# Dilated attention in a hybrid decoder layer: far scores by residue class on column tiles, value products ahead of scores

## What is computed

```python
DIL_PAIRS = ((128, 1), (512, 4), (2048, 16))

def dilated_attention(q, k, v):
    """For pair (w, r) a query at t attends t, t-r, t-2r, ..., t-w.
    Branch outputs are merged with weights proportional to their softmax denominators."""
    for window, dil in DIL_PAIRS:
        o, lse = banded_causal_attention(to_stream(q), to_stream(k), to_stream(v), window // dil)
        ...
    w = jax.nn.softmax(jnp.stack(lses), axis=0)
    o = jnp.einsum('pbsh,pbshd->bshd', w, jnp.stack(outs).astype(jnp.float32))
```

## Time and profile before

| | |
|---|---|
| median of 3 runs | 507.02 us (506.67 to 508.36) |
| the profiled execution | 507.9 us, of it the span 505.4 us |
| PE busy | 489.3 us, 97% |
| DVE, ACT, POOL busy | 310.9, 227.4, 72.7 us |
| largest parts of PE's chain | output products (line 954) 16%, value products (line 913) 10%, input projection (lines 776 to 778) 24% |

### The profile page before, as it was taken

One profiled execution on the slowest core, in us unless ns is written; L12 is line 12 of the kernel. 1 busy time (PEld: TensorE's weight loads), 2 busy tenths in 40 slices (PEclk: granted clock), 3 DMA queues, 4 the chain that ended last, 5 costly groups with the idle time before them and its releaser, 6 DMA issues.

```text
span 505.4 us, 9699 instructions
## 1 busy us (share of the span) xinstructions
PE 489.3 (97%) x3480; PEld 448.2 (89%) x3480; DVE 310.9 (62%) x889; ACT 227.4 (45%) x512; POOL 72.7 (14%) x53
## 2 busy tenths in 40 slices
PE   4999999999999999999999999999999999999993
PEld 4999999999999988888888888899888888888882
DVE  4776645557574853434534468876767867787634
ACT  5633123112121134564545669946474655554640
POOL 0000000000000000111011100023232323231425
PEclk9999999999999999999999999999999999999998
DMA  8957272538633244432331357823342424241022
GB/s 284 377 160 205 89 245 83 172 122 266 210 110 112 95 138 134 133 94 90 95 95 49 97 173 238 247 58 105 110 137 63 149 56 151 64 145 45 3 81 83
DMA packets 51710, 67.82 MB, mean 134 GB/s; under 512 B 9553, under 2 KB 41297, under 8 KB 51665
## 3 DMA queue, kind: packets, MB, share of 16 engines
q1 hardware_dynamic: 51088, 66.17, 41.6%
q10 hardware_dynamic: 576, 1.05, 0.6%
HBM read 51.18 MB, written 16.02 MB: 133 GB/s over the span
## 4 chain that ended last, share of the span: by engine, by line
PE 90%; DMA 3%; DVE 3%; SPq 1%; ACT 1%; issue 1%; POOLq 0%; POOL 0%; ACTq 0%; DVEq 0%
PE long_ps L954 16%; PE o_ps L913 10%; PE wide L777 8%; PE wide L776 8%; PE wide L778 8%; PE long_ps L853 5%; PE long_ps L855 5%; PE wide L881 5%; PE narrow L893 5%; PE long_ps L854 5%; PE wide L882 4%; DMA q_pair<-q_spill 2%; PE wide L788 1%; PE wide L787 1%; PE wide L789 1%; PE narrow L931 1%
## 5 line engine op out<-in xcount | busy, mean ns | idle before, releaser
L776 PE MATMUL wide<-x_hi,w_hi 128*128 128x256 f32 x320 | 89.5, 280 | 0.3 <-DVE w_lo L1188 0.3
L777 PE MATMUL wide<-x_lo,w_hi 128*128 128x256 f32 x320 | 89.7, 280 | 0.0
L778 PE MATMUL wide<-x_hi,w_lo 128*128 128x256 f32 x320 | 89.4, 279 | 0.0
L776 PEld LDWEIGHTS wide<-x_hi,w_hi 128*128 128x128 f32 x320 | 60.2, 188 | 0.5 <-issue 0.4
L777 PEld LDWEIGHTS wide<-x_lo,w_hi 128*128 128x128 f32 x320 | 60.1, 188 | 0.0
L778 PEld LDWEIGHTS wide<-x_hi,w_lo 128*128 128x128 f32 x320 | 59.9, 187 | 0.0
L1035 ACT ACTIVATE spill<-turn 128x512 fp32r<-128x512 f32 x21 | 13.3, 632 | 103.3 <-DVE turn L1270 76.6
L1517 POOL TENSOR_TENSOR g_lo<-g_raw,g_hi 128x1024 fp32r<-128x1024 f32 x6 | 14.3, 2388 | 272.7 <-ACT g_hi L1040 272.7
L954 PE MATMUL long_ps<-wo_hi,y_hi 128*128 128x512 f32 x128 | 53.1, 415 | 0.0
L954 PE MATMUL long_ps<-wo_lo,y_hi 128*128 128x512 f32 x128 | 52.3, 408 | 0.0
L954 PE MATMUL long_ps<-wo_hi,y_lo 128*128 128x512 f32 x128 | 51.8, 404 | 0.0
(11 more groups left out here) (158 smaller groups left out, 1227.2 us busy)
## 6 DMA issues: line engine op xcount, KB each, us to landing
q_spill<-spill SPq DMA_DIRECT2D x32, 256.0 KB, 2.5
q_pair<-q_spill SPq DMA_DIRECT2D x128, 64.0 KB, 2.0
w_raw<-in_w_qkv SPq DMA_DIRECT2D x12, 512.0 KB, 5.3
x_raw<-in_x_t SPq DMA_DIRECT2D x16, 256.0 KB, 8.0
g_raw<-in_w_gate SPq DMA_DIRECT2D x8, 512.0 KB, 3.5
q_pair<-q_spill SPq DMA_DIRECT2D x32, 128.0 KB, 2.8
q_pair<-q_spill SPq DMA_DIRECT2D x128, 32.0 KB, 1.8
wo_raw<-in_w_out SPq DMA_DIRECT2D x8, 512.0 KB, 4.4
```

Source lines behind the costliest of these rows:

```text
L776: pe.matmul(dst, w_hi[s][:, k, f], t_hi[:, k, cols], start=(k == 0), stop=False)
L777: pe.matmul(dst, w_hi[s][:, k, f], t_lo[:, k, cols], start=False, stop=False)
L778: mm = pe.matmul(dst, w_lo[s][:, k, f], t_hi[:, k, cols], start=False, stop=(k == KT - 1))
```

## The change

- `score`: the far keys get products of their own, four per unit, one per class: 32 query columns (`q_whole`, unsplit fp32) times the keys of that class, read from k_b with a step of four elements, on the column tile of that class. Far and dense scores go to one PSUM bank, far ones first.
- POOL makes `q_whole` by adding the two halves of the query (`join_queries`), at the end of iteration v for unit v + 1; PE waits for it (`q_joined`).
- DVE masks far columns already in merged form with a mask that is gathered beforehand; the merge and its semaphore go.
- far value groups are cut at 96 rows where there are more than 128 (block 7: 96 and 96 instead of 128 and 64).
- `times_v(v - 3)` moves from the end of iteration v to its start, ahead of the scores, and `unit_out` of DVE follows (unit v - 3 instead of v - 4); the last block's stages move up by one iteration. The far values of unit u then stand directly ahead of the far scores of unit u + 2.

```diff
@@ -100,6 +100,8 @@
 UB = len(UNITS) // NB
 CLASSES, CP = 4, P // 4
 FAR = {4: 3, 5: 4, 6: 4, 7: 6}
+FAR_ROWS = 3 * CP
+FAR_COLS = SEQ // CLASSES
 QO = 6
 
 
@@ -129,7 +131,7 @@
 
 def branch_done(i, j):
 
-    return max(u for u, unit in enumerate(UNITS) if unit[0] == "abc"[j] and unit[1] == i) + 4
+    return max(u for u, unit in enumerate(UNITS) if unit[0] == "abc"[j] and unit[1] == i) + 3
 
 
 
@@ -145,7 +147,6 @@
           {i: OUT_AT[i] + n for i, n in enumerate(OUT_ITERATIONS)}]
 STATS_AT = RES_AT[1]
 NORM_AT = {i: v + 1 for i, v in RES_AT[1].items()}
-NORM_AT[NB - 2] = YSPLIT_AT[NB - 1, 2]
 for table in (RMS_AT, Y_AT, YSPLIT_AT, NORM_AT):
     assert [table[key] for key in sorted(table)] == sorted(table.values())
 ITERATIONS = max(NORM_AT.values()) + 1
@@ -201,11 +202,8 @@
 def key_chunks(u):
 
     kind, _, _, heads, nk = UNITS[u]
-    if kind != "b":
-        return [(0, C * (heads - 1) + nk * P)]
-    if far_tiles(u):
-        return [(0, far_groups(u)[0][1] * P), (far_groups(u)[0][1] * P, nk * P)]
-    return [(c, min(c + HALF, nk * P)) for c in range(0, nk * P, HALF)]
+    far = far_tiles(u)
+    return [(0, far * CP + (nk - far) * P if kind == "b" else C * (heads - 1) + nk * P)]
 
 
 def far_tiles(u):
@@ -216,8 +214,8 @@
 
 def far_groups(u):
 
-    n = far_tiles(u)
-    return [(at, min(4, n - at)) for at in range(0, n, 4)]
+    n = far_tiles(u) * CP
+    return [n] * (n > 0) if n <= P else [FAR_ROWS, n - FAR_ROWS]
 
 
 def two_tiles(u):
@@ -867,20 +864,28 @@
                     pe.wait_ge(narrow_read[last % 2], last // 2 + 1)
                 if u >= 2:
                     pe.wait_ge(probs_ready, u - 1)
-                for c, (lo, hi) in enumerate(key_chunks(u)):
-                    _, bank = bank_of(wide, plan.wide, ("scores", u, c))
-                    for hh in range(heads):
-                        h = h0 + hh
-                        if kind == "a":
-                            dst = bank[:, hh * C:hh * C + nk * P]
-                            keys = k_a[:, h // (HA // GA), (i + 1 - nk) * P:(i + 1) * P]
-                        elif kind == "b":
-                            dst, keys = bank[:, 0:hi - lo], k_b[:, h, lo:hi]
-                        else:
-                            dst, keys = bank[:, hh * C:(hh + 1) * C], k_c[:, h, :]
-                        pe.matmul(dst, q[:, hh, 0:P], keys, start=True, stop=False)
-                        mm = pe.matmul(dst, q[:, hh, P:2 * P], keys, start=False, stop=True)
-                    mm.then_inc(wide_full, 1)
+                _, bank = bank_of(wide, plan.wide, ("scores", u, 0))
+                far = far_tiles(u)
+                if far:
+                    f = far_index[u]
+                    pe.wait_ge(q_joined, f + 1)
+                    for c in range(CLASSES):
+                        rows = slice(c * CP, (c + 1) * CP)
+                        pe.matmul(bank[rows, 0:far * CP], q_whole[:, f % 2, rows],
+                                  f32(k_b[:, h0, c:far * P:CLASSES]), start=True, stop=True,
+                                  tile_position=(0, c * CP))
+                for hh in range(heads):
+                    h = h0 + hh
+                    if kind == "a":
+                        dst = bank[:, hh * C:hh * C + nk * P]
+                        keys = k_a[:, h // (HA // GA), (i + 1 - nk) * P:(i + 1) * P]
+                    elif kind == "b":
+                        dst, keys = bank[:, far * CP:far * CP + (nk - far) * P], k_b[:, h, far * P:nk * P]
+                    else:
+                        dst, keys = bank[:, hh * C:(hh + 1) * C], k_c[:, h, :]
+                    pe.matmul(dst, q[:, hh, 0:P], keys, start=True, stop=False)
+                    mm = pe.matmul(dst, q[:, hh, P:2 * P], keys, start=False, stop=True)
+                mm.then_inc(wide_full, 1)
 
             def transpose_probs(u):
                 pe.wait_ge(probs_ready, u + 1)
@@ -966,6 +971,8 @@
 
             filler(0, 0)
             for v in range(ITERATIONS):
+                if 0 <= v - 3 < n_units:
+                    times_v(v - 3)
                 if 0 <= v - 1 < n_units:
                     score(v - 1)
                 if 0 <= v - 2 < n_units:
@@ -975,8 +982,6 @@
                 for i, j in stage_at(v, Y_AT):
                     transpose_y(i, j)
                 filler(v, 1)
-                if 0 <= v - 3 < n_units:
-                    times_v(v - 3)
 
 
         @block.scalar
@@ -1085,12 +1090,10 @@
                         act.wait_ge(narrow_full, probs_turn(u - 2) + 1)
                 if u >= 4:
                     act.wait_ge(o_done, u - 3)
-                if far_tiles(u):
-                    act.wait_ge(far_merged, merges(u))
                 for hh in range(heads):
                     cols = slice(hh * P, (hh + 1) * P) if kind == "a" else slice(hh * C, hh * C + nk * P)
-                    if far_tiles(u):
-                        cols = slice(HALF - (nk - far_tiles(u)) * P, HALF + far_tiles(u) * CP)
+                    if kind == "b":
+                        cols = slice(*key_chunks(u)[0])
                     src = prob[s][:, cols]
                     if from_bank:
                         src = bank[:, hh * C + P:(hh + 1) * C] if kind == "a" else bank[:, cols]
@@ -1402,35 +1405,26 @@
                     dve.wait_ge(mask_b_in, 16)
                     for n in plan.turned[-2:]:
                         dve.wait_ge(*spills(n))
-                for c, (lo, hi) in enumerate(key_chunks(u)):
-                    dve.wait_ge(wide_full, plan.wide["scores", u, c] + 1)
-                    _, bank = bank_of(wide, plan.wide, ("scores", u, c))
-                    if kind == "b":
-                        off = (NB - nk) * P
-                        to = lo
-                        if far_tiles(u):
-                            to = HALF if c == 0 else HALF - (hi - lo)
-                        ttr = dve.tensor_tensor_reduce(prob[s][:, to:to + hi - lo], bank[:, 0:hi - lo],
-                                                       mask_b[:, off + lo:off + hi], 1.0, -3e38, ALU.add, ALU.max,
-                                                       mx[:, s, c:c + 1])
...
+                dve.wait_ge(wide_full, plan.wide["scores", u, 0] + 1)
+                _, bank = bank_of(wide, plan.wide, ("scores", u, 0))
+                if kind == "b":
+                    far = far_tiles(u)
+                    parts = [(0, (NB - nk) * CP, far * CP)] if far else []
+                    parts.append((far * CP, FAR_COLS + HALF - (nk - far) * P, (nk - far) * P))
+                    for part, (lo, off, n) in enumerate(parts):
+                        ttr = dve.tensor_tensor_reduce(prob[s][:, lo:lo + n], bank[:, lo:lo + n],
+                                                       mask_b[:, off:off + n], 1.0, -3e38, ALU.add, ALU.max,
+                                                       mx[:, s, part:part + 1])
...
                 ttr.then_inc(row_max, 1)
                 dve.wait_ge(row_max, masked_index[u] + 1)
                 if kind == "b":
-                    dve.tensor_reduce(nb[:, r, 0:1], mx[:, s, 0:len(key_chunks(u))], AX.X, ALU.max, negate=True)\
+                    dve.tensor_reduce(nb[:, r, 0:1], mx[:, s, 0:len(parts)], AX.X, ALU.max, negate=True)\
                        .then_inc(neg_max, 1)
-                    done = merges(u) - len(far_groups(u))
-                    for g, (first, n) in enumerate(far_groups(u)):
-                        if g:
-                            dve.wait_ge(far_merged, done + g)
-                        at_col = HALF if g == 0 else 0
-                        dve.tensor_reduce(prob[s][:, HALF + g * P:HALF + g * P + n * CP],
-                                          prob[s][:, at_col:at_col + n * P].rearrange("p (j c) -> p j c", c=CLASSES),
-                                          AX.X, ALU.max).then_inc(far_merged, 1)
                 else:
                     dve.tensor_reduce(lows[:, h0 // 2, :, 0], mx[:, s, :].unsqueeze(2), AX.X, ALU.max, negate=True)\
                        .then_inc(first_lows, 1)
@@ -1461,8 +1455,8 @@
             dve.wait_ge(negated, 3)
             dve.wait_ge(mask_a_in, 48)
             for v in range(ITERATIONS):
-                if 0 <= v - 4 < n_units:
-                    unit_out(v - 4)
+                if 0 <= v - 3 < n_units:
+                    unit_out(v - 3)
                 if 0 <= v - 1 < n_units:
                     unit_max(v - 1)
                 if 0 <= v - 2 < n_units and two_tiles(v - 2):
@@ -1517,6 +1511,14 @@
                 pool.tensor_tensor(g_lo[f % 2][:, :, :], g_raw[f % 2][:, :, :], f32(g_hi[f % 2][:, :, :]),
                                    ALU.subtract).then_inc(gate_split, 1)
 
+            def join_queries(u):
+
+                f, q = far_index[u], q_pair[u % QS]
+                if f >= 2:
+                    pool.wait_ge(wide_full, scores_turn(next(w for w in far_index if far_index[w] == f - 2)) + 1)
+                pool.wait_ge(*queries(u))
```

(37 more changed lines are left out.)

8 lines of the change are left out of this document (1 added, 7 removed).

## The result

The changed kernel takes 516.97 us (median of 6 runs, 511.7 to 518.46), the kernel before 506.99 in the same job: a ratio of 1.0181, with an interval of 1.0145 to 1.0218. That is 10.0 us slower, where I had written 5.7. The profiled execution took 516.99 us, its span 515.2. The range that I had given was 509.3 to 516.5 us, so the median lies 0.5 us above its upper end.

A forecast was written before the change was run, and what follows sets the result against it. PE, busy 97% of the span, was taken to bound the kernel; -2.0 (scores) + 2.6 - 0.9 (earlier values) + 6.0 (POOL wait) = +5.7 us gave 512.7 us, range 509.3 to 516.5 for 8 in 10.

The forecast's parts named there:

- the clock: Rival: PE's clock falls in one of the two long POOL waits, costing 2.3 us, for 515.0 us; chance 0.10.
- part 1: PE's far score products: -7.8 us old columns, +3.6 new columns, +2.2 fixed; sum -2.0 us, bounds -4.6 and +1.3.
- part 3: PE's far scores wait for POOL's q_whole behind the layer norm: 2.7 us at unit 63, 3.3 at 71; +6.0 us.
- part 2: Value products one iteration sooner make PE wait for turned probabilities from DVE and ACT: +2.6 us, less 0.9 of present waits.
- the price of a column: Far score tiles on PE: 0.83 ns per unsplit fp32 column, between 0.45 and 1.9; 4,352 columns make 3.6 us.
- the 0.55: Far score set on PE, expected about 0.35 us to the first dense product; 0.55 us or more would make the prediction wrong.
- the first rival: Far scores on PE: key stream with a step runs at half pace, 3.6 us more, 516.3 us; chance 0.13.
- the fixed part: Far score sets on PE: 0.14 us per set besides its columns, 16 sets, 2.2 us; vanishes at the high column price.
- The switches: PE changing between full array and column tiles around far values and scores: taken as 0, between -1.0 and +0.8 us.
- the many small waits: Expected sign: PE shows many small waits for the writes of prob_t, in block 3 for ACT's.

The follow-up runs named there:

- experiment 9: Changed kernel with joins at the start of POOL's iteration, dilated-branch keys and values sorted by class, and value products back behind the fillers: 505.10 us, ratio to before 0.9961.
- experiments 8 and 9: Both: changed kernel, joins first, dilated-branch keys and values sorted by class. The former keeps values ahead of scores, 505.83 us; the latter puts them behind the fillers, 505.10 us.
- experiment 7: The kernel before with only the value products and DVE's division moved earlier (and the last block's stages); scores, merges and masks as before: 521.07 us, ratio 1.0281.

## Why the prediction was right in direction and too small

The loss adds up from differences of medians: waits for POOL +5.4, the clock +1.8, the step of four +3.9, the values moved +1.2, the class-by-class products without the step -2.3 (10.0 less the other four, so a remainder; experiment 9 has -1.9 for them, with the sorting in it), together +10.0 us. The measured time is 4.3 us above the forecast: +3.6 from part 1, +1.8 from the clock, -0.6 from part 3, -0.5 from part 2. By the prediction's own steps:

- **Part 3, the wait for POOL**, forecast +6.0 us: right. Two waits, at units 63 and 71, as named, 5.4 us together by the medians, 2.59 and 2.50 by the rows of PE, against 2.7 and 3.3. For unit 71 I had taken PE and the norm as unmoved; in the changed kernel ACT's pass ahead of the norm starts 4.2 us before PE asks (448.55 and 452.73), before the change 3.45 us (441.34 and 444.79). The other 14 joins cost nothing, as assumed.
- **Part 1, the score products**, forecast -2.0: without the step right to 0.3 us (-2.3), with it +1.6. The term that was mis-sized is the price of a column, 0.83 ns, which I had chosen between 0.45 ns and the 1.9 that the far value products allow; their operands are read without a step. Without the step of four it holds: a set of 128 columns takes 0.33 us, forecast 0.35, and the sets of 192 take 0.44 to 0.46, forecast 0.46 (0.14 + 384 x 0.00083). With the step a column takes 1.8 ns and the 128-column set 0.57 us, which is past the 0.55 that I had named as the sign of being wrong. I had this as the first rival, by the Trainium skill's rule, with the price of 3.6 us (measured 3.9), and gave it 0.13. My reason against it, that an fp32 column has slack in its read, was argued from a duration, not from a row with a step, and was wrong. A rule that names the very pattern of the change should have weighed more than that. (The lower bound of part 1, -4.6, was summed wrong: at 0.45 ns a column the fixed part is 0.19 us and not 0.14, which makes -3.8. No rival changes by it.)
- **The switches**, forecast 0 (between -1.0 and +0.8): not measured by themselves. In the changed kernel the far scores start 0.14 us behind the start of the value set (439.07 to 439.21), where before the next full product came 0.25 us behind it; 0.11 us less at 12 such places would be 1.3 us, an estimate. "TensorEngine Tiling (Array Packing)" of the Trainium skill, section "Key Properties", has it so: a change of mode drains the array, a change of tile does not, and the trace agrees. All the same, of the kernels of experiments 8 and 9, which differ by this order, the one that has values and scores together is 0.7 us slower: the order brings the waits for prob_t with it.
- **Part 2, values one iteration sooner**, forecast +2.6 less 0.9: net 1.2 us with the switches in it. The reasoning (DVE's write 0.93 us late at such a place, of which the lost merge and the shorter mask give back 0.8) is borne out by experiment 7: where they don't go, there are 12 waits of 0.8 us on average. The size was too large: in place of the many small waits that I had named, PE shows two for prob_t in the changed kernel, 0.8 us together, and with the join first five, 1.5 us, against 2.6. What rests on both halves of the change comes to 1.2 us; the move without the new scores costs 14.
- **The clock**, a rival with 0.10 and +2.3 us: it came, and not once but twice, and cost 1.8 together. Its sign and place were right; it should have been part of the forecast, as the waits were forecast at about the 3.1 us of rest that the end of the trace shows ahead of the lower clock. The price from the start of the trace (5.40 us of products that would take 3.1) was too high here, where fewer columns run in the stretch and a part of them fills a wait.

So two of the rivals came true together with the forecast. The sum of the three, 512.7 + 3.6 + 2.3, would have been 518.6, nearer to 516.97 than the forecast alone; I had treated as exclusive what adds up.

## What to carry to other kernels

Where PE streams an fp32 operand with a step that leaves one element in 16 bytes, either sort the data once or count the read at half pace (1.8 against 0.86 ns a column here); a step of 8 bytes was nearly free. A small producer that an in-order engine puts behind long background work belongs at the head of the queue: a join of 0.45 us behind 4.8 us of layer norm made up 7.2 of 10.0 us, and moving two lines took it away. And two parts of a change can carry each other: the earlier value products cost 1.2 us with the new scores and 14 us without, so neither can be priced, kept or dropped by itself.

## What the runs showed of the hardware

- PE streaming fp32 keys through 32-column tiles: 1.8 ns a column and pass (four classes side by side) with a step of 16 bytes, 0.86 without a step, and 0.47 us against 0.44 for a whole set of 192 with 8 bytes against none. Runs of 128 bytes that lie 512 bytes apart go as fast as unbroken ones (0.44 us for both; 0.46 where the set is entered from the full array).
- The clock's fall does not sit on the end of the wait. At unit 71 it came before PE was at work again (0.92 for 452.50 to 455.20), at unit 63 after it: PE starts at 423.15, and the row below still has the full clock; the row from 424.10 on has 0.50. Twenty products of 256 columns in the wait of 2.6 us kept the clock at full.

```profile
423.20:424.00 0.80, 0.80 (x9) 0.39 (x10) 0.00 (x0) 0.00 (x0) 0.22 (x1) 1.00 0.00 0
```
